# Second feed-forward as seven block products with weight sums on GpSimd; attention's scaling and the first norm rearranged

## What is computed

```python
def rms_norm(x, g):
    return x * lax.rsqrt(jnp.mean(x * x, axis=-1, keepdims=True) + EPS) * g

def modulate(x, g, shift, scale):
    return rms_norm(x, g) * (1 + scale) + shift

def swiglu(h, w_gate, w_up, w_down):
    return (jax.nn.silu(h @ w_gate) * (h @ w_up)) @ w_down

for l in range(2):
    mod_lat = s_lat @ ada_w[l] + ada_b[l]          # six vectors of 1024
    sh1, sc1, g1, sh2, sc2, g2 = jnp.split(mod_lat, 6, axis=-1)
    out_lat = mixer_l(modulate(x, norm_mix_g[l], sh1, sc1), ...)
    x = x + g1 * out_lat
    x = x + g2 * swiglu(modulate(x, norm_ffn_g[l], sh2, sc2), ffn_w_gate[l], ffn_w_up[l], ffn_w_down[l])
```

## Time and profile before

| | |
|---|---|
| median of 3 runs | 1633.02 us (1632.67 to 1634.59) |
| the profiled execution | 1633.62 us |
| its span | 1631.8 us |
| PE busy | 1590.9 us, 97% of the span |
| DVE busy | 990.9 us, 61% |
| ACT busy | 650.1 us, 40% |
| POOL busy | 87.5 us, 5% |
| mean granted TensorE clock | 0.997 |

### The profile page before, as it was taken

One profiled execution on the slowest core, in us unless ns is written; L12 is line 12 of the kernel. 1 busy time (PEld: TensorE's weight loads), 2 busy tenths in 40 slices (PEclk: granted clock), 3 DMA queues, 4 the chain that ended last, 5 costly groups with the idle time before them and its releaser, 6 DMA issues.

```text
span 1631.8 us, 26012 instructions
## 1 busy us (share of the span) xinstructions
PE 1590.9 (97%) x10120; PEld 1373.0 (84%) x10120; DVE 990.9 (61%) x1580; ACT 650.1 (40%) x1191; POOL 87.5 (5%) x151
## 2 busy tenths in 40 slices
PE   5999999999999999999999999999999999999999
PEld 4888877678799899899989977888887888888887
DVE  5697778543796388358638666877664533343334
ACT  4344444451643144124314343556683422322222
POOL 0431010010000000000000100101000000000000
PEclk9999999999999999999999999999999999999999
DMA  9633310462122312422231431111135233233333
GB/s 363 70 100 104 128 42 27 184 243 64 52 79 101 133 52 72 162 78 78 100 133 53 152 109 53 40 53 39 53 121 201 78 109 110 102 119 100 108 111 103
DMA packets 49493, 170.51 MB, mean 104 GB/s; under 512 B 5584, under 2 KB 5712, under 8 KB 49264
## 3 DMA queue, kind: packets, MB, share of 16 engines
q1 hardware_dynamic: 37104, 127.00, 23.1%
q10 hardware_dynamic: 7984, 28.31, 4.8%
q0 software_dynamic: 4304, 13.80, 2.9%
HBM read 164.87 MB, written 4.19 MB: 104 GB/s over the span
## 4 chain that ended last, share of the span: by engine, by line
PE 89%; DVE 5%; ACT 3%; issue 1%; DMA 1%; SPq 0%; ACTq 0%; DVEq 0%
PE PS L684 38%; PE PS L2722 9%; PE PS L2509 8%; PE PS L2382 6%; PE PS L2378 6%; PE PS L2379 6%; PE PS L2552 2%; PE PS L2316 2%; PE PS L2340 1%; DMA scr<-in_ada 1%; PE PS L2449 1%; DVE c_early L1846 1%; PE PS L2570 1%; PE PS L2808 1%; PE PS L2809 1%
## 5 line engine op out<-in xcount | busy, mean ns | idle before, releaser
L648 DVE TENSOR_TENSOR w_lo<-raw,w_hi 128x1024 fp32r<-128x1024 f32 (+2 forms) x172 | 190.9, 1110 | 130.4 <-ACT w_hi L642 127.6
L642 ACT ACTIVATE w_hi<-raw 128x1024 fp32r<-128x1024 f32 (+2 forms) x172 | 165.4, 962 | 220.9 <-PE PS L684 155.5
L684 PE MATMUL PS<-c_hi,w_hi 128*128 128x512 f32 (+1 forms) x672 | 203.6, 357 | 1.0 <-DVE c_lo L1566 0.6
L684 PE MATMUL PS<-c_lo,w_hi 128*128 128x512 f32 (+1 forms) x672 | 202.3, 355 | 0.0
L1541 DVE SCALAR_TENSOR_TENSOR X<-PS,mod,X 128x512 f32<-128x512 f32 (+2 forms) x120 | 75.8, 659 | 197.7 <-PE PS L684 191.8
L684 PE MATMUL PS<-c_hi,w_lo 128*128 128x512 f32 (+1 forms) x672 | 152.1, 355 | 0.0
L684 PE MATMUL PS<-h_hi,w_hi 128*128 128x512 f32 x368 | 139.0, 385 | 0.9 <-ACT scr L885 0.6
L684 PE MATMUL PS<-h_lo,w_hi 128*128 128x512 f32 x368 | 138.9, 385 | 0.0
L684 PEld LDWEIGHTS PS<-c_hi,w_hi 128*128 128x128 f32 x672 | 110.7, 188 | 21.0 <-issue 1.2
L1846 DVE SCALAR_TENSOR_TENSOR c_early<-X,small,c_early 128x798 f32<-128x798 f32 x120 | 125.9, 1050 | 2.9
L684 PEld LDWEIGHTS PS<-c_lo,w_hi 128*128 128x128 f32 x672 | 110.5, 188 | 18.8
(11 more groups left out here) (387 smaller groups left out, 3081.9 us busy)
## 6 DMA issues: line engine op xcount, KB each, us to landing
raw<-in_w SPq DMA_DIRECT2D x152, 512.0 KB, 3.3
adaw<-in_ada ACTq DMA_DIRECT2D x28, 512.0 KB, 4.2
adaw<-in_w SPq DMA_DIRECT2D x20, 512.0 KB, 4.4
scr<-in_ada POOLq DMA_DIRECT2D x19, 512.0 KB, 8.6
raw<-in_w SPq DMA_DIRECT2D x24, 384.0 KB, 3.1
h_early<-in_ada SPq DMA_DIRECT2D x12, 512.0 KB, 6.1
scr<-in_ada ACTq DMA_DIRECT2D x12, 512.0 KB, 5.7
scr<-in_ada SPq DMA_DIRECT2D x4, 1024.0 KB, 15.0
```

Of the source, the lines that this page charges most:

```text
L642: nc.scalar.activation(w_hi[:, j, 0:tiles], raw[:, j].rearrange("p (k n) -> p k n", k=KT)[:, 0:tiles], ACT.Copy).then_inc(s_hi, 1)
L648: nc.vector.tensor_tensor(w_lo[:, j, 0:tiles], raw[:, j].rearrange("p (k n) -> p k n", k=KT)[:, 0:tiles], w_hi[:, j, 0:tiles].bitcast(f32) ...
L684: last = nc.tensor.matmul(G[j][:, a:b], w[:, j, k], m[:, k, a:b], start=(n == 1), stop=(n == 3 * k_tiles))
```

## The change

Three parts.

1. **Second feed-forward.** 20 of the 22 pairs of gate and up tiles are made as seven block products, now 4 feature tiles x 3 passes x 256 columns (`stream_block`). They are chained in PSUM: in a pair's first bank products 1, 6, 7 and 4 are added one on the other, in its second 5 and 3, in its third 2. ACT copies what is needed between two links (`copied_1`, `copied_5`, `copied_u2`), DVE adds a bank and a copy (`gate_0`, `gate_1`, `up_1`) and multiplies by the silu (`gated_0`, `gated_1`), all 256 wide. PE's order is 1, 5, 4 of the pair before, 6, 3, 2, 7. The four weight sums of a pair (128 x 512) are made by POOL. Sums of activations are made once, by DVE; ACT writes a whole copy of the eight latent tiles in the norm ahead (`h_whole`). At a group's end the down weight takes the place of the next pair's, product 4 of the last pair is made within the first down product, and DVE's `up_1` comes behind `split_lo` of the down weight, `gate_0` and `lo` of product 4.
2. **Attention.** For units U below 16 POOL multiplies the probabilities by the inverted row sum in place (one `tensor_tensor` for each head, 128 x 512, 448 or 256), the diagonals are not made, and PE's turns are `transpose` against `ident`. The masks come one head at a time between these. `ab_product` runs the passes with w_hi first, and waits for w_lo behind them.
3. **Start.** ACT and DVE square X in turn into eight buffers, and PE sums all eight (8 x 512 and 8 x 256 columns, float32) against ones from a memset. Only `ident` (64 KB) is loaded of the constants behind part 0 of the modulation weights, the two weight tiles come behind part 1, and the rest of the constants last. `first_quarter` takes the place of `first_pair`: w_hi passes first, then w_lo.

```diff
+            pool.wait_ge(s_h, 48)
+            pool.wait_ge(s_adm, 96)
+            for q in range(NB, 2 * NB):
+                a0, a1, u0, u1 = (four(chunk(q, c)[:, n:n + 512]) for c in range(2) for n in (0, 512))
+                for c in range(2):
+                    pool.wait_ge(s_pw[q % 2][c], 16 * (q // 2) + 16)
+                if q >= NB + 2:
+                    pool.wait_ge(s_bl, BLOCK_AT[q - 2, 7])
+                nc.gpsimd.tensor_tensor(SUM_7[q % 2], a0, u0, ALU.subtract).then_inc(s_sb, 1)
+                pool.wait_ge(s_sb, 4 * q + 1)
+                nc.gpsimd.tensor_tensor(u0, u0, u1, ALU.add).then_inc(s_sb, 1)
+                pool.wait_ge(s_sb, 4 * q + 2)
+                pool.wait_ge(s_bl, BLOCK_AT[q, 1])
+                nc.gpsimd.tensor_tensor(a0, u0, a0, ALU.subtract).then_inc(s_sb, 1)
+                pool.wait_ge(s_sb, 4 * q + 3)
+                if q >= NB + 2:
+                    pool.wait_ge(s_bl, BLOCK_AT[q - 2, 3])
+                nc.gpsimd.tensor_tensor(SUM_3[q % 2], a1, a0, ALU.subtract).then_inc(s_sb, 1)
...
 ACT:
+                    for q in range(first, end):
+                        last = q + 1 == end
+                        if q > first:
+                            stream_hi(act, q - 1, 4)
+                        copied_1(q)
+                        stream_hi(act, q, 6)
+                        copied_5(q)
+                        stream_hi(act, q, 3)
...
+                        stream_hi(act, q, 2)
+                        copied_u2(q)
+                        stream_hi(act, q, 7)
+                        if q > first:
+                            pair_hi(q - 1, q - 1 + tile)
+                        silu_1(q)
+                        if not last:
+                            stream_hi(act, q + 1, 1)
+                        else:
+                            act.wait_ge(s_bp, BLOCK_AT[q, 5])
+                            split_hi(act, R // 2, 0, tiles=nf)
+                        silu_0(q)
+                        if not last:
+                            stream_hi(act, q + 1, 5)
+                        else:
+                            stream_hi(act, q, 4)
+                    pair_hi(q, q + tile)
...
 DVE:
+                        if q > first:
+                            up_1(q - 1)
+                            stream_lo(dve, q - 1, 4)
+                            gated_1(q - 1)
+                        stream_lo(dve, q, 6)
+                        stream_lo(dve, q, 3)
...
+                        if q > first:
+                            gated_0(q - 1)
+                        stream_lo(dve, q, 2)
+                        stream_lo(dve, q, 7)
+                        if q > first:
+                            hidden_lo(q - 1 + tile, q - 1 + tile - f0)
...
+                        gate_1(q)
+                        if not last:
+                            stream_lo(dve, q + 1, 1)
+                        else:
+                            split_lo(dve, R // 2, 0, tiles=nf)
+                        gate_0(q)
+                        if not last:
+                            stream_lo(dve, q + 1, 5)
+                        else:
+                            stream_lo(dve, q, 4)
+                    up_1(q)
+                    gated_1(q)
+                    gated_0(q)
+                    hidden_lo(q + tile, q + tile - f0)
...
 PE:
+                    for q in range(first, end):
+                        stream_block(q, 1)
+                        stream_block(q, 5)
+                        if q > first:
+                            stream_block(q - 1, 4)
+                        for b in (6, 3, 2, 7):
+                            stream_block(q, b)
...
+                    for k in range(nf - 1):
+                        if k == 3:
+                            stream_block(end - 1, 4)
+                        down_pass(k, w_hi, c_hi, nf)
+                        down_pass(k, w_hi, c_lo, nf)
+                    if nf - 1 <= 3:
+                        stream_block(end - 1, 4)
+                    pe.wait_ge(s_lo, R + 1)
+                    for k in range(nf - 1):
+                        down_pass(k, w_lo, c_hi, nf)
+                    pe.wait_ge(s_hid, hid)
...
 attention:
+            def scaled(U):
+                nk = keys(U)
+                pool.wait_ge(s_rr, U + 1)
+                for h in (1, 0):
+                    p = Pb[:, U % 2, h, 0:nk]
+                    nc.gpsimd.tensor_tensor(p, p, tmp(3, U, h).to_broadcast([128, nk]), ALU.mult).then_inc(s_Ps, 1)
...
+                        if U < SCALED:
+                            last = nc.tensor.transpose(dst, p, ident)
+                        else:
+                            last = MM(dst, p, dg[:, U % 2, h], start=True, stop=True)
...
 start:
+            pe.wait_ge(s_eps, 2)
+            for k, (dve_made, act_count, dve_count) in enumerate(SQ0):
+                if dve_made:
+                    pe.wait_ge(s_nacc, dve_count)
+                else:
+                    pe.wait_ge(s_nsq, act_count)
+                for a, b in BOTH:
+                    last = MM(SSA[:, a:b], ones_0, sq0[k][:, a:b], start=(k == 0), stop=(k == KT - 1))
```

More of the change, by code:

```diff
@@ L49, with block_stream @@
 R_F1 = R_O1 + 8
-NP = R_F1 + 2 * FT + 32
-NR = NP + 2 * (FT - PLAIN)
+NP = R_F1 + 2 * PLAIN + 32
+NB = FT - PLAIN
+NR = NP + 4 * NB
+def block_stream():
+    at, n = {}, 7 * NB
+    for f, end in zip(FIRST, PAIRS):
+        for q in range(NB + f, NB + end):
+            for b in (1, 5, 4, 6, 3, 2, 7):
+                if b != 4 or q > NB + f:
+                    n += 1
+                    at[q - (b == 4), b] = n
+        n += 1
+        at[NB + end - 1, 4] = n
+    return at
+BLOCK_AT = block_stream()
 SM = {}
@@ L561, in _, with masks @@
             pool.wait_ge(s_zero, 4)
-            def masks(hp):
+            def masks(hp, heads):
                 if hp:
                     pool.wait_ge(s_mx, 8 * hp)
-                for h in range(2):
+                for h in heads:
                     H, b = 2 * hp + h, bx[h]
@@ L985, in ffn, with gate_silu @@
             def ffn():
[L987 to L989 removed]
+                R, half = R_F1, R_F1 // 2 + 1
+                def gate_silu(half):
                     act.wait_ge(s_gemm, 2 * half + 1)
@@ L992, in hidden, with hidden_hi @@
                     nc.scalar.activation(sg[:, 0:LAT], G[0][:, 0:LAT], ACT.Silu).then_inc(s_gf[0], 1)
[L993 to L996, removed]
-                for g, (f0, nf) in enumerate(GROUPS):
[L999 to L1002, removed]
-                        split_hi(act, half, 1)
-                        hidden(half, i)
-                    R += 2 * nf
+                def hidden_hi(at):
+                    nc.scalar.activation(c_hi[:, at, 0:LAT], ftmp[:, 0:LAT], ACT.Copy).then_inc(s_hhi, 1)
@@ new lines, in gate_0, with gate_1 @@
+                def gate_0(q):
+                    dve.wait_ge(s_bp, BLOCK_AT[q, 2])
+                    dve.wait_ge(s_sn, q + 1)
+                    if q == NB:
+                        dve.wait_ge(s_gf[1], half + 1)
+                    else:
+                        dve.wait_ge(s_f, 2 * q)
+                    V.tensor_tensor(sg[:, 0:LH], chained(q, 2), p1s[:, 0:LH], ALU.add).then_inc(s_g0, 1)
+                def gate_1(q):
+                    dve.wait_ge(s_bp, BLOCK_AT[q, 3])
+                    dve.wait_ge(s_u2, q + 1)
+                    if q == NB:
+                        dve.wait_ge(s_gf[1], half + 1)
+                    else:
+                        dve.wait_ge(s_f, 2 * q - 1)
+                    V.tensor_tensor(sg[:, LH:LAT], chained(q, 3), u2c, ALU.add).then_inc(s_g1s, 1)
```

369 lines of the change are left out of this document (291 added, 78 removed).

## The result

The changed kernel takes 1646.55 us (median of 4 runs, 1643.88 to 1648.06), the kernel before 1632.85 beside it: a ratio of 1.0077, interval 1.0061 to 1.0093 (the quotient of the two medians is 1.0084, inside it). It is 13.7 us slower. The forecast was 1628, range 1608 to 1640.

What follows compares the result with a forecast made beforehand. The prediction took PE as the bound, busy for 97% of the span. From 1633.6 us it added 6.7 for feed-forward and norm, took off 8.8 for attention and 3 for the start: 1628.5, or 1628 against the median; range 1608 to 1640.

Steps and rivals of the forecast that it cites:

- PE's own work: Second feed-forward: a pair takes PE 10.08 us instead of 10.88, saving 16 us over 20 pairs.
- I take 0.7 us a pair: Second feed-forward: delay when POOL's weight sums lock out DVE's operations in the ACT-DVE loop; bounds 0 to 1.5 us.
- the loop of 10.8: Second feed-forward: pair-to-pair time through ACT and DVE, 10.1 us plus 0.7 for POOL's sums, against 10.88 before.
- rival E: Second feed-forward: POOL starts late on a pair behind its transfer, period 11.2 to 11.6 us, total 1641; chance 0.12.
- 10.1 us of walk: Second feed-forward: summed ACT and DVE steps from product 5 to the next pair's, as long as PE's work.
- The signs named for it: Second feed-forward's expected profile: pairs of 10.8 us, waits on ACT's hi, DVE's lo mean above 0.69, maximum near 1.7.
- A: The forecast itself: feed-forward loop about 10.8 us, attention gives half its saving; range 1623 to 1633, chance 0.42.
- Ends of groups: Second feed-forward, last pair of each group: PE waits 1.6 us for DVE, four times, +6.6; last group +1.3 more.
- +6.4 in the sum: Whole second feed-forward without the norm: -4.5 for pairs, +6.6 and +1.3 at group ends, +3 at its start.
- Start of the feed-forward: Second feed-forward's beginning: activation sums and first block weights through POOL and ACT cost +3 us (0 to 5).
- Attention: Attention: half of PE's saving from cheaper turns survives POOL's multiplies locking out DVE, -8.8 us (-14.4 to +2).
- Start: Kernel's start: modulation weights land 3.5 us earlier and PE's wait of 3.65 goes, -3 us (-5 to 0).

Runs made afterwards that it cites:

- experiment 2: Changed kernel with a third buffer for a pair's weights in groups of six, so transfers wait less: 1650.88 us, ratio 1.0090 to the kernel before.
- experiment 4: Changed kernel with POOL's sums narrowed to 64 columns, plus four full POOL subtractions a pair that nobody waits for: 1662.78 us, ratio 1.0179.
- experiment 5: Changed kernel with weight sums on DVE, and at group ends up_1 and gate_0 earlier on DVE, hi of 4 earlier on ACT: 1615.92 us, ratio 0.9887.
- experiment 7: Kernel before with only the attention's and start's changes, probabilities scaled by ACT, not POOL: 1619.47 us, ratio 0.9896 (0.9940 with POOL).

## Why the prediction was wrong, step by step

- **PE's own work**, 10.05 to 10.08 us a pair: right; undisturbed products follow each other at 1.44 us (1419.40 - 1407.70 holds seven of them and the waits), and in the kernel with the sums on DVE the second step of each later group is 9.97.
- **The step that failed: "I take 0.7 us a pair" for POOL's sums, and with it the loop of 10.8.** Measured were 11.47, and 10.19 where the sums are narrow and all else is as it was, so the full sums cost 1.28 us a pair. Two things were in it. The lock was priced as two chance meetings in the loop of ACT and DVE. The runs show the two engines taking turns once both have work: 2.9 us in a row in experiment 2, and 2.4 us a pair for work that nobody waits for in experiment 4. In the changed kernel the held-up lo of product 4 and the held-up sum also lie in the loop through the transfer, where the forecast put nothing (only rival E did). And a sum costs 1.27 us and not 1.05: the row of before is that of a multiply of 112 partitions whose two inputs are both read as broadcasts. An undisturbed multiply with one broadcast input in the attention is 1.04 for 512 columns too. Whether the operands or the operation make the difference was not tried. An estimate by the ratio in the Trainium skill, "GPSIMD Engine Reference", section "Performance versus the Vector engine", would have been 1.34 us. Measured alone it is 1.27 / 0.68 = 1.87 times, and the page was nearer than the row that I took.
- **The clock**, which the forecast left out: of the twelve steps the one with the clock at half is 14.3, 3 us over the mean of the others, and so some 3 of the 8 us by which the period missed.
- **Rival E**, held at 0.12, had the mechanism that the changed kernel shows: lo of product 4, transfer, two sums, hi of 5, a period of 11.2 to 11.6 and 1641 in all. Its sums are less (3.0 together, not 4.0). The transfer with what follows until POOL starts is more (4.9 to 5.1, not 4.4), and so is DVE's way through up_1 and a held up lo of 4 (2.6 to 2.9 from the end of the hi of 5 to the transfer). I held it too low since I weighed transfer and port one by one; they act together, as the port lengthens both the sums and the lo at the loop's two ends. That 10.1 us of walk had nothing left over was said in the prediction and should have counted against a value under 11. The signs named for it came all the same: waits on ACT's hi before product 5, a longer lo (1085 ns from `raw`, at most 1.8 us) and sums of 1.48 on the mean. They would have been there with a loop of 10.8 too, so they could not tell A from E.
- **Ends of groups**, 1.6 us each: right in place and nearly in size, 1.84 in three groups and 1.3 in the last, with DVE's up_1 as the one waited for; experiment 5 gave it back. What was missed is that the last pair of a group also has the loop's wait: from its first product to product 4 it takes 14.8, and 17.0 in the first group, where the sum had 13.1. That is 9 us, the largest single error beside the period's 12 x 0.67 = 8; the 17.0 has one of the three stretches at half clock in it. With the start of the feed-forward (next point) these two make up the miss of this part: +6.4 in the sum, +24.8 measured.
- **Start of the feed-forward**, +3: 13.29 against 8.6 for six products is 4.7, with the later groups at 0.7 to 0.8 for the same.
- **Attention**, -8.8: -8.0, and the mechanism as it was put, DVE's convolution steps beside POOL (1139 for 1049 ns) with half of PE's saving used up; experiment 7 returned 3.5 of it.
- **Start**, -3: -1.0 in this trace; the first matmul behind it is at 51.6 to 52.8 in all kernels with the new start, and at 52.9 and 53.4 in the two with the old. The 25.48 us step came at 22.26, as said, and PE's eight sums ended at 19.4 where 19.8 was said. But PE then waits for ACT, which has four h_hi and w_hi ahead of the copy for the next modulation part, and the first matmuls run slow behind the wait: two of them (512 and 256 columns) take 0.64 us, where 0.35 is usual, at a granted clock of 0.59 between 27.27 and 31.00. PE's rows, and that stretch:

```profile
22.26 1.95 PE L2642 MATMUL PS<-scr,sT 128*32 128x128 f32 x64
...
27.27 0.39 PE L2649 MATMUL PS<-const,scr 128*128 128x8 f32 x2 [3.06 <-ACT scr L1250]
...
27.96 0.84 PE L2854 MATMUL PS<-h_lo,w_hi 128*128 128x512 f32 x2
28.60 0.84 PE L2854 MATMUL PS<-h_hi,w_hi 128*128 128x512 f32 x2
...
27.27:31.00 3.73, 3.73 (x14) 3.20 (x15) 3.70 (x8) 0.90 (x1) 0.00 (x0) 0.59 1.03 412
```

- The Trainium skill's page "SBUF — State Buffer", section "SBUF: two separate sides", says that the loser of the port waits for the whole instruction, and names DVE operations with two inputs in SBUF among those that take it. The rows of experiment 2 agree: 0.42 for up_1, with one input in PSUM, beside a sum, 1.51 for gated_1. How often the two meet is for the traces to say. Four full meetings at the 0.84 us of the earlier trace rows would be 3.4 us a pair; experiment 4 shows 2.4 of period, so that count is an upper bound, and mine of 0.7 was too low.

## What to carry to other kernels

When GpSimd is to take elementwise work from VectorE, take one full instruction of waiting for each of its instructions as the upper bound, as soon as VectorE has a queue of two-input operations (here 0.6 us of period for each), and price the sum by an instruction with the same kind of operands. Where a walk over two engines is as long as the bound's own work, no stall of it is free. With narrow sums the transfer was hidden (10.19), and the port alone was not (12.64 with the idle work). Look at the granted clock before explaining the last few microseconds between two traces: 2 us of a lead and 5 of a loss lay there. And an order at the end of a loop deserves its own look: two swaps in VectorE's order and one in ScalarE's were worth 0.57% of the kernel.

## Not expected of the hardware

POOL and DVE take turns while both have work: in experiment 2 POOL's sums of 1.27 us end 1.4 to 1.75 us apart, and DVE's two-input instructions of 0.42 and 0.69 take 1.46 to 1.75, one after each. GpSimd's multiply with a broadcast input took 1.04 us for 512 columns undisturbed and 0.61 for 256, its subtraction of two full tensors 1.27 for 512. ScalarE did the same multiply in place with a per-row scale, 19 us more of work in the attention, and the attention was 3.5 us shorter than with GpSimd's.
